# Where two groups of small transfers are issued: nine first loads without their wait, and the last two stores from another engine's queue

## The reference, cut to what matters

```python
for l in range(DEPTH):
    sh1, sc1, g1, sh2, sc2, g2 = adaln_params(cond, w_ada[l], b_ada[l])    # silu(cond) @ w_ada + b_ada
    q_na, k_na, v_na, q_mla, c_kv, k_r, gate_na, gate_mla = mixer_inputs(modulate(x, sh1, sc1), ...)
    y = merge_branches(o_na, o_mla, gate_na, gate_mla, *out_w)
    x = layer_norm(ALPHA * x + g1 * y, ln1_g[l], ln1_b[l])
    y = hierarchical_moe(modulate(x, sh2, sc2), *moe_w)                    # 32 experts, 2 per token
    x = layer_norm(ALPHA * x + g2 * y, ln2_g[l], ln2_b[l])
return x of both groups, and k, v and latents of the prompt
```

## Time and profile before

| | us |
|---|---|
| median of three runs | 1120.14 |
| lowest and highest run | 1115.66, 1121.81 |
| profiled execution, its own time | 1115.66 |
| its span, from the first to the last instruction | 1113.9 |
| PE busy | 974.7 (88%) |
| DVE, ACT, POOL busy | 328.5, 231.9, 30.2 |
| moved by DMA | 324.60 MB, 290 GB/s over the span |

### The profile page before, as it was taken

How to read it: one execution, slowest core, us unless ns; L and a number is a source line. 1 busy time by engine, 2 the same in 40 slices (tenths; PEclk the granted TensorE clock), 3 DMA queues, 4 the chain that set the end, 5 groups by cost and what they waited for, 6 DMA issues and landing times.

```text
span 1113.9 us, 15645 instructions
## 1 busy us (share of the span) xinstructions
PE 974.7 (88%) x6820; PEld 592.4 (53%) x6820; DVE 328.5 (29%) x748; ACT 231.9 (21%) x475; POOL 30.2 (3%) x56
## 2 busy tenths in 40 slices
PE   4999899999886898978879999999988889897875
PEld 1888667778432333324249876777863233432421
DVE  2122333126531212112170133322374121311116
ACT  1102315101320212112121041331024121211111
POOL 1100000000000000000010000000000000000000
PEclk9899999999888999999889999999988999999888
DMA  9939854655429999999875336664532699999970
GB/s 383 404 138 372 342 199 152 231 187 228 177 85 417 422 429 430 428 430 425 372 298 230 139 113 270 275 267 171 204 152 114 248 429 429 432 427 429 420 323 38
DMA packets 38526, 324.60 MB, mean 291 GB/s; under 512 B 4920, under 2 KB 5048, under 8 KB 9392
## 3 DMA queue, kind: packets, MB, share of 16 engines
q1 hardware_dynamic: 33696, 308.82, 67.8%
q0 software_dynamic: 4320, 13.28, 3.4%
q10 hardware_dynamic: 432, 1.39, 0.3%
HBM read 321.05 MB, written 2.42 MB: 290 GB/s over the span
## 4 chain that ended last, share of the span: by engine, by line
PE 73%; DMA 11%; DVE 7%; ACT 5%; issue 3%; SPq 1%; DVEq 0%; ACTq 0%
PE ps L761 12%; PE ps L659 9%; PE ps L810 8%; PE ps L685 6%; DMA expert_gate_up<-in_w_gu 6%; PE ps L774 5%; PE ps L865 5%; PE ps L937 5%; PE ps L950 5%; DMA expert_down<-in_w_dn 3%; PE ps L588 3%; PE ps L718 3%; PE ps L609 2%; PE ps L820 2%; DMA dense<-in_w_ada 2%
## 5 line engine op out<-in xcount | busy, mean ns | idle before, releaser
L761 PE MATMUL ps<-expert_gate_up,gathered_prompt 128*32 128x512 f32 x768 | 170.6, 597 | 17.4 <-DMA expert_gate_up<-in_w_gu 15.0
L761 PE MATMUL ps<-expert_gate_up,gathered_sample 128*32 128x512 f32 x768 | 170.6, 598 | 0.0
L810 PE MATMUL ps<-expert_down,hiddenT 128*32 128x512 f32 x1024 | 117.4, 602 | 13.8 <-ACT gathered_sample L1139 4.5
L761 PEld LDWEIGHTS ps<-expert_gate_up,gathered_prompt 128*32 128x32 f32 x768 | 50.5, 110 | 125.8 <-issue 123.2
L659 PE MATMUL ps<-hT,dense 128*128 128x256 f32 x512 | 114.2, 381 | 0.0
L659 PEld LDWEIGHTS ps<-hT,dense 128*128 128x128 f32 x512 | 96.1, 190 | 15.4 <-issue 2.5
L1557 DVE SCALAR_TENSOR_TENSOR y_lo<-ps,slot_weight,y_hi 128x512 fp32r<-128x512 f32 x64 | 48.0, 751 | 106.6 <-ACT y_hi L1171 106.6
L810 PEld LDWEIGHTS ps<-expert_down,hiddenT 128*32 128x32 f32 x1024 | 33.1, 110 | 83.6 <-issue 59.7
L1540 DVE TENSOR_TENSOR hidden<-hidden,ps 128x256 f32<-128x256 f32 x32 | 13.4, 420 | 210.1 <-ACT hidden L1155 210.1
L685 PE MATMUL ps<-dense,hT 128*128 128x256 f32 (+1 forms) x320 | 66.8, 372 | 1.7 <-ACT hT L1096 1.7
L588 PE MATMUL ps<-dense,cond 128*32 128x256 f32 x768 | 54.0, 411 | 15.4 <-ACT cond L1193 11.7
(11 more groups left out here) (217 smaller groups left out, 1102.9 us busy)
## 6 DMA issues: line engine op xcount, KB each, us to landing
expert_gate_up<-in_w_gu SPq DMA_DIRECT2D x64, 2048.0 KB, 18.4
expert_down<-in_w_dn SPq DMA_DIRECT2D x64, 1024.0 KB, 14.4
dense<-in_w_ada SPq DMA_DIRECT2D x48, 1024.0 KB, 8.9
dense<-in_w_in SPq DMA_DIRECT2D x28, 1024.0 KB, 8.9
dense<-in_w_o SPq DMA_DIRECT2D x8, 1024.0 KB, 5.1
dense<-in_w_out SPq DMA_DIRECT2D x8, 1024.0 KB, 4.8
dense<-in_w_c SPq DMA_DIRECT2D x4, 1024.0 KB, 25.4
gate<-ada_rows POOLq DMA_DIRECT2D x4, 1024.0 KB, 8.5
```

The lines of the kernel that those rows point to most:

```text
L761: last = mm(ps[r0:r0 + 32, q, :], xg[s][:, k, at_:at_ + CAP], w_gu[(i * EPI + 2 * q + j) % SLOTS][:, k, :], start=(k == 0), stop=(k == KD ...
L810: last = mm(ps[32 * e:32 * e + 32, banks[c], :], h, w_dn[(i * EPI + e) % SLOTS][:, f, c * 512:(c + 1) * 512], start=(f == 0), stop=(f == 1 ...
```

## The change

Three places of the program differ. The wait for `ada_used` at 7 ahead of POOL's nine small loads of layer 0 is gone. The two stores of `x_res` are no longer issued by SP but by POOL, after everything else that POOL issues, with the same waits for `x2_ready`. The wait for these stores to land is now POOL's too.

```diff
@@ block.sync
-            for s in range(2):
-                sp.wait_ge(x2_ready, 2 * (DEPTH - 1) + s + 1)
-                sp.dma_start(io["x_out"][:, s, :], x[:, s, :]).then_inc(x_stored, 16)
-            sp.wait_ge(x_stored, 32)
@@ block.gpsimd
                 if l:
                     pool.wait_ge(*reached(M[l - 1], "sc_filled", 2 * ITERS))
                     pool.wait_ge(y_read, 2 * l)
-                else:
-                    pool.wait_ge(ada_used, 7)
                 pool.dma_start(qn[:, :], dram(io["q_norm"], l * QL, [[0, P], [1, QL]])).then_inc(small_in, 16)
...
+            for s in range(2):
+                pool.wait_ge(x2_ready, 2 * (DEPTH - 1) + s + 1)
+                pool.dma_start(io["x_out"][:, s, :], x[:, s, :]).then_inc(x_stored, 16)
+            pool.wait_ge(x_stored, 32)
             pool.wait_ge(k_stored, 16 * DEPTH)
```

## The result

| | before | after |
|---|---|---|
| median of 8 runs, us | 1119.31 (1115.66 to 1121.81) | 1124.89 (1123.00 to 1127.89) |
| ratio of after to before | 1 | 1.0056, interval 1.0040 to 1.0073 |
| granted clock, profiled execution | 0.955 | 0.946 |

The two medians lie 5.6 us apart (0.50%); the forecast was +5.8 us. The ratio that came with these runs is not the quotient of these two medians: it is 1.0056, which is 6.3 us, with an interval from 4.5 to 8.2 us.

The account below looks back on a forecast made before the run. The prediction took the start to be bound by the eighth w_ada unit's landing with full DMA engines, then by PE. 5.2 us there plus 0.6 at the last stores, added to 1120.14, gave 1125.9 us, range 1119.8 to 1129.8.

Parts of the forecast that it names:

- The frame: At the start, the eighth w_ada unit's landing sets the end; with full DMA engines, bytes put ahead delay it.
- part one: At the start, POOL's nine loads without their wait go ahead of the eighth w_ada unit: 5.2 us later, within 4.0 to 6.3.
- signs: Marks in the changed profile that part one is right, such as eighth unit at 32 to 34 us, projection at 37 to 39.
- The upper bound: For part one at the start: short rows cost twice what they cost in the earlier profile, 6.3 us.
- The bound from bytes alone: For part one at the start: the nine loads' 1.71 MB at 430 GB/s cost 4.0 us.
- "I add nothing" for the clock: Ahead of the projection, TensorE's lower clock (0.50) stays since PE waits even longer for the eighth unit; nothing added.
- The shift was kept: From the projection through the expert load near 333 us to the end, all 5.2 us of delay stay.
- swallowed at 333 us: Rival: the expert load's wait near 333 us takes up the start's delay, leaving 0.6 us, 1120.7 us; chance 0.09.
- The stall of POOL: In POOL's early loads, about seven transfers can be outstanding; the two behind them start at 20 to 22 us.
- that rival: At the start, three queues starve ACT's, x_res lands over 4 us later; some 2 us more, 1128 us; chance 0.07.
- Part two: At the kernel's end, x_res stores from POOL instead of SP finish 0.6 us later, within -0.3 to 1.5.
- The sum: Over the whole kernel, 5.2 plus 0.6 makes 5.8 us slower, with 3.7 and 7.8 as ends.

Follow-up runs that it names:

- e1: The kernel before with only POOL's wait for ada_used at 7 removed, stores still with SP; ratio 1.0041 (1.0025 to 1.0057).
- e3: The kernel before with POOL's wait for ada_used at 8 in place of 7; ratio 0.9997 (0.9982 to 1.0012).
- e4: The kernel before with POOL's wait for ada_used at 4 in place of 7; ratio 1.0008 (0.9991 to 1.0026).
- e8: The kernel before with half of x_res and most of const loaded behind the eighth w_ada unit, sample's hT later, POOL's wait at 8; ratio 0.9987 (0.9977 to 0.9998).
- the five kernels with a like start: The kernel before, e2, e3, e7 and e11, with POOL's wait at 7 or 8 and nothing else changed at the start; eighth unit begins at 27.64 to 27.91 us.
- e2: The kernel before with only the x_res stores and the wait for their landing moved to POOL; ratio 1.0005 (0.9986 to 1.0024).
- e7: The kernel before with the two x_res stores and their wait moved to ACT; single run, span ended 3.0 us after DVE.
- e11: The kernel before with the x_res stores issued by POOL while SP waits for their landing; single run, span 1112.7 us.
- e5: The kernel before with seven of POOL's nine loads going without the wait, cache_kr and router_b kept behind it; ratio 1.0025 (1.0007 to 1.0043).
- e6: The kernel before with only cache_kr and router_b going without the wait, the other seven loads kept behind it; ratio 0.9994 (0.9977 to 1.0010).

## Why the prediction was right

**The frame held.** The eighth unit's landing sets the start, the engines are full there, and whatever goes ahead delays it. e1, e3, e4 and e8 show it: +6.1, +0.1, +2.2 and -1.7 us at the eighth unit, against the mean of 27.81, for all, nothing and part of POOL's traffic ahead of it, and for less of ACT's.

**The size of part one was low.** I took 5.2 us from the engines' share of POOL's queue in the earlier trace rows, within 4.0 to 6.3. Measured at the eighth unit it is 6.1 us in e1 and 7.2 in the kernel after; the latter is beyond my bound, and so are the eighth unit at 34.99 and the projection at 40.03, where I had set 32 to 34 and 37 to 39 as signs. The upper bound was also short by its own rule: the short rows' extra was 5.4 - 4.0 = 1.4 us, and twice that on top of the bytes is 6.8 (6.6 with the same 0.2 taken off), not 6.3. The queue's own share after, 5.9 us with `ada_bias`, is nearer. The bound from bytes alone was far off the value, because 36 KB in short rows cost 1.1 to 1.4 us, as much as the low rates in the earlier trace rows had suggested.

What the sum left out stands in the row of SP's own queue. From 0 us until PE begins the eighth unit, in the kernel before and in the kernel after:

```profile
q1 hardware_dynamic: 1242, 9.13, 81.2%
```

```profile
q1 hardware_dynamic: 1319, 9.69, 67.8%
```

The eight units are 8.39 MB; the rest is units behind the eighth, of which some packets move before the eighth's last one. In the five kernels with a like start SP's queue has moved 9.11 to 9.18 MB by then, in e1 9.35, in the kernel after 9.69, in e4 only 8.87. At 430 GB/s these differences from 9.14 are +0.5, +1.3 and -0.6 us. Added to POOL's share less `ada_bias` (5.6 us in e1, 5.7 after, 2.7 in e4) they give 6.1, 7.0 and 2.1, against 6.1, 7.2 and 2.2 measured. With full engines such a sum has to come out, so it says where the time went, not why: of the 1.1 us between e1 and the kernel after, 0.8 are packets of later units. Why one execution sends more of them first stays open.

**"I add nothing" for the clock can stand, with a spread.** The reason given, a longer wait ahead of the eighth unit, did not come: PE waited 1.41 us there instead of 2.30, and 3.34 us ahead of the seventh. The clock was at its lower level all the same, and the unit took 1.98 us again. In the profiled execution after, the 7.35 us at the projection's start were 6.6 at its end, since the projection took 32.24 us instead of 33.00. The clock rose at another point. Before, the stretch from 34 to 36 us still had this:

```profile
34.00:36.00 2.00, 2.00 (x10) 1.70 (x10) 0.00 (x0) 0.02 (x1) 0.00 (x0) 0.94 1.02 425
```

In the kernel after, the projection's first full stretch has the full clock:

```profile
40.00:42.00 2.00, 1.97 (x9) 1.77 (x10) 1.13 (x4) 1.37 (x4) 0.00 (x0) 1.00 1.00 421
```

With a start like that of the kernel before the projection took 33.00, 34.1 (e2, e7), 32.8 (e3) and 32.24 us (e11), and with a late one 32.24 (after, e5), 32.6 (e1) and 32.9 (e4). Late starts seem to have it a little shorter, but the two groups overlap; whether the change gives something back here stays open.

**The shift was kept in the main**, as forecast: in e1, set against the one trace of the kernel before, 5.9, 5.6 and 5.7 us at the projection's end, the expert wait and the end. Against the mean of the five at the expert wait (333.98) it is 5.0 us in e1, 5.4 in e5 and 7.9 in the kernel after, but 1.5 in e4 and -0.7 in e6. The rival "swallowed at 333 us" falls; the load was issued behind PE there again.

**The stall of POOL came sooner than forecast.** It stopped ahead of `kcT`, not `vc` alone, and `vc` went at 24.32 and not at 20 to 22. That about seven transfers can be outstanding is too simple a reading: `q_norm` had landed at 13.4 us and let nothing through, while `vc` went 0.4 us after `router_b` had landed, at 23.9 now and at 40.7 before. What the rule is, the runs don't show. `cache_ckvT` landed at 24.85 + 8.9 = 33.8, still ahead of the eighth unit. `x_res` landed 1.8 us later (14.9 to landing against 13.1), within the 3.5 that I had allowed; that rival falls too.

**Part two was low, within its bounds.** I forecast 0.6 us (-0.3 to 1.5), from 0.3 at the issue and 0.3 to landing. These measured 0.27 (0.30 less SP's 0.03) and 0.4. A third item was missing from the sum: POOL also waits for the landing, and that cost 0.45 us (e11).

**The sum.** 6.1 to 7.2 plus 1.15 makes 7.2 to 8.3 us at the two places of the change by the profiled executions; the ratio says 6.3, within 4.5 to 8.2, and the two medians lie 5.6 apart. Both of my terms were low by the trace, and that 5.8 met 5.6 so closely is partly luck. The ratio falls short of the trace in every version with traffic ahead: 4.6 against 6.1 us in e1, 0.9 against 2.2 in e4, 2.8 against 5.0 in e5, -0.7 against 1.4 in e6, 6.3 against 8.3 after. Each of these gaps is within or near the timing's interval, but all point one way, so 1 to 2 us may be given back behind the eighth unit. The clock at the projection's head could do that; the runs leave it open.

## What to carry to other kernels

A wait that holds small transfers back can be worth more than it costs, when what lands first sets the start: ask not who waits for a transfer, but what it is put ahead of. Price such a transfer by the engines' share in the queue's row and not by its bytes: here the two with short rows cost over ten times what their bytes say, at the point where the engines were full. The last store belongs on a queue whose engine wakes quickly, here SP's or ACT's, and so does the wait for its landing.

## What the runs showed of the hardware that I had not expected

- POOL is slower to notice a semaphore than SP: 0.30 against 0.03 us from DVE's end to the issue, and 0.45 us more between a store's landing and the end of the span (e11, a single run).
- 256 rows of 128 and 160 bytes, 36 KB in all, held up the eighth `w_ada` unit, on another queue, by 1.1 to 1.4 us.
- The same 160 products of the projection took 32.2 to 34.1 us in kernels whose start is alike, as TensorE's clock came back from its lower level (1.2 of 2.4 GHz) sooner or later; and in six of thirteen traces it fell again near 120 to 130 us, after a wait for the softmax: in all those with a projection of 32.24 or 34.1 us and in none with 32.6 to 33.0. That the two go together is only seen, not tested. Single traces differ by 1 to 2 us at each of these places, and gains of 1.5 us at the start could not be found in the timing.
